# A fused encoder layer on one core: the even-block sums of a pair of products are made ahead of the decay scan

## What is computed

```python
h = rmsnorm(x, gains[2])
z = h @ w_in
q, fz, iv, og, u, ga, gb = jnp.split(z, IN_SPLITS, axis=-1)
logf = jnp.logaddexp(jnp.log(lb_h), jnp.log1p(-lb_h) + jax.nn.log_sigmoid(fz))
k = (1.0 - lb_h) * jax.nn.sigmoid(-fz)
# in chunks of 64 tokens, per head:
G = jnp.cumsum(gc, axis=-2)
o_inter = jnp.einsum('bhtk,bhkv->bhtv', qc * jnp.exp(G), S)
att = jnp.einsum('bhtk,bhsk,bhtsk->bhts', qc, kc, decay)
S_new = jnp.exp(G_last)[..., None] * S + einsum(kc * jnp.exp(G_last - G), vc)
```

## Time and profile before

| what | value |
|---|---|
| median of 3 runs | 2341.67 us (2340.02 to 2345.33) |
| the profiled execution | 2344.26 us |
| its span | 2342.5 us |
| TensorE busy, matmuls | 2270.4 us, 97% |
| VectorE busy | 1580.9 us, 67% |
| ScalarE busy | 1267.5 us, 54% |
| GpSimd busy | 1343.3 us, 57% |
| scans (line 2750) | 8, the first at 736.3, the last at 1119.3 us |

### The profile page before, as it was taken

The page is one execution under the profiler, slowest core; times in us unless marked ns, Lnnn a source line. Parts: engine busy times, 40 slices in busy tenths (PEclk is TensorE's granted clock), DMA queues, the critical chain, the costliest instruction groups (busy, mean ns, idle before and its releaser), DMA issues.

```text
span 2342.5 us, 54526 instructions
## 1 busy us (share of the span) xinstructions
PE 2270.4 (97%) x20432; PEld 1951.9 (83%) x20432; DVE 1580.9 (67%) x2618; ACT 1267.5 (54%) x2295; POOL 1343.3 (57%) x1019
## 2 busy tenths in 40 slices
PE   8899999999898999999999999999999999999998
PEld 6688888888787888888878888877888888888886
DVE  7877767635589788888982332389687777445755
ACT  6454555433576666666554434564555554334775
POOL 2787777767614555555645444306777778677120
PEclk9999999999999999999999999999999999999999
DMA  3123222443430111111121212331232222536202
GB/s 132 50 85 100 90 79 86 148 146 103 160 104 23 40 40 48 48 40 41 45 60 36 63 59 75 116 102 33 82 99 83 86 77 86 181 119 199 71 19 75
DMA packets 155236, 194.93 MB, mean 83 GB/s; under 512 B 13168, under 2 KB 102512, under 8 KB 155120
## 3 DMA queue, kind: packets, MB, share of 16 engines
q1 hardware_dynamic: 111920, 153.59, 20.7%
q10 hardware_dynamic: 43200, 39.83, 5.2%
HBM read 155.49 MB, written 37.88 MB: 83 GB/s over the span
## 4 chain that ended last, share of the span: by engine, by line
PE 72%; DVE 12%; POOL 5%; ACT 4%; issue 4%; DMA 2%; SPq 1%; ACTq 0%; DVEq 0%; POOLq 0%
PE bank L1069 18%; PE bank L1072 18%; PE bank L1071 18%; PE bank L1036 4%; PE bank L1038 4%; PE bank L1037 4%; POOL ring L930 2%; DVE hid L2204 2%; DMA ring<-weights 2%; POOL ring L934 1%; PE bank L1169 1%; DVE ops L2259 1%; DVE ops L2212 1%; DVE hid L2358 1%; PE bank L1204 1%
## 5 line engine op out<-in xcount | busy, mean ns | idle before, releaser
L1069 PE MATMUL bank<-ops,ring 128*128 128x264 f16 x4112 | 1138.0, 277 | 20.5 <-DVE ops L2368 7.4
L1071 PE MATMUL bank<-ops,ring 128*128 128x264 f16 x4112 | 1137.3, 277 | 0.0
L1072 PE MATMUL bank<-ops,ring 128*128 128x264 f16 x4112 | 1137.2, 277 | 0.0
L930 POOL TENSOR_TENSOR ring<-ring 128x512 f16<-128x512 f32 (+1 forms) x492 | 666.1, 1372 | 278.3 <-ACT ring L1404 278.3
L1404 ACT ACTIVATE ring<-ring 128x512 f16<-128x512 f32 (+1 forms) x492 | 286.4, 614 | 504.7 <-POOL ring L934 502.3
L1069 PEld LDWEIGHTS bank<-ops,ring 128*128 128x128 f16 x4112 | 404.0, 98 | 89.7 <-DVE ops L2368 8.5
L1072 PEld LDWEIGHTS bank<-ops,ring 128*128 128x128 f16 x4112 | 403.2, 98 | 61.2
L1071 PEld LDWEIGHTS bank<-ops,ring 128*128 128x128 f16 x4112 | 403.2, 98 | 59.9
L915 POOL TENSOR_TENSOR ring<-wtmp,ring 128x512 f16<-128x512 f32 x107 | 131.0, 1229 | 340.0 <-ACT ring L1345 339.4
L1036 PE MATMUL bank<-hid,ring 128*128 128x264 f16 x1068 | 294.9, 276 | 1.5 <-issue 1.3
L1038 PE MATMUL bank<-hid,ring 128*128 128x264 f16 x1068 | 294.8, 276 | 0.0
(11 more groups left out here) (227 smaller groups left out, 3627.5 us busy)
## 6 DMA issues: line engine op xcount, KB each, us to landing
ring<-weights SPq DMA_DIRECT2D x363, 256.0 KB, 2.8
ops<-spill SPq DMA_DIRECT2D x16, 1056.0 KB, 7.2
ring<-weights SPq DMA_DIRECT2D x120, 128.0 KB, 2.5
spill<-hid ACTq DMA_DIRECT2D x42, 264.0 KB, 2.9
spill<-hid ACTq DMA_DIRECT2D x20, 528.0 KB, 5.0
ops<-spill SPq DMA_DIRECT2D x8, 792.0 KB, 5.6
hid<-xT SPq DMA_DIRECT2D x8, 528.0 KB, 8.2
hid<-out_x ACTq DMA_DIRECT2D x8, 528.0 KB, 8.7
```

The costliest lines, as they stand in the source:

```text
L930: nc.gpsimd.tensor_tensor(low(slot, kh), weight_source(name, k, kh), high(slot, kh), ALU.subtract)\
L1069: nc.tensor.matmul(out, whi, xhi, start=(kk == 0 and fresh(name, k)), stop=False, skip_group_check=True)
L1071: nc.tensor.matmul(out, whi, xlo, start=False, stop=False, skip_group_check=True)
L1072: mm = nc.tensor.matmul(out, wlo, xhi, start=False, stop=end, skip_group_check=True)
```

## The change

On VectorE, in every turn but the first, the two sums of product 6 of the pair before now stand ahead of the wait for the logarithm and of the scan. The other engines' streams are the same.

```diff
+                if not (isinstance(h, int) and h == 1):
+                    sums_b_even("heads", h * 2 - 3, in_tokens(V))
                 dve.wait_ge(logf_ready, hh + 1)
                 V_.tensor_tensor_scan(GG, smask, W[2], 0.0, ALU.mult, ALU.add).then_inc(cum_ready, 1)
                 if isinstance(h, int) and h == 1:
                     t_lows(1, 4)
 
                     dve.wait_ge(t_ready, 14)
-                if not (isinstance(h, int) and h == 1):
-
-                    sums_b_even("heads", h * 2 - 3, in_tokens(V))
                 dve.wait_ge(cum_ready, hh + 1)
```

## The result

The changed kernel takes 2345.62 us in the median of 20 runs, the kernel before 2341.38 in 20 runs; the ratio is 1.0019 with a 95% interval of 1.0011 to 1.0026. Three of the forty runs (one before, two changed) were slow, at 2946 us and more; the ratio leaves them out, and without them the medians are 2345.01 and 2341.22. So the changed kernel is slower, by 3.8 to 4.2 us in the medians, which is 0.2%; the interval says 2.6 to 6.1 us.

What follows compares the result with a forecast made beforehand. TensorE (PE) bounds the kernel, busy 97% of the span and all 54.18 us of a head turn. Losses of 2.0 + 0.45 + 0.73 + 0.78 = 4.0 us on the 2341.67 median give 2345.7, range 2342.2 to 2348.0.

Steps and rivals of the forecast that it cites:

- Where the sums go: VectorE at the head seam: second sum starts 0.38 us after product 6's last matmul; V-transpose waits vanish, 1.4 us won.
- the lower bound: Changed turns gain their waits at the V transposes and lose nothing: -1.4 us.
- What is queued behind it: VectorE's scan, behind a sum waiting for PE, starts 1.08 us late; the difference L2760 starts 0.50 us late.
- Who waits for L2760: ACT, then POOL (4.32 us later), whose port lock sets the K operand's end (2.31 later); K-transpose wait 0.73 a turn.
- The sum: Turns 2 to 8 lose 2.0 + 0.45 + 0.73 + 0.78 = 4.0 us, won waits already set off.
- A turn: Sign of being right: one turn of the head loop takes 54.7 us in place of 54.18.
- B: Only VectorE's queue passes the delay to the K operand: 2.1 us slower, 2343.8; chance 0.17.
- C: K operand gets the shared port before POOL, both transpose waits vanish: 1.2 us faster, 2340.5; chance 0.09.
- D: L2760's bare wait on the scan's end costs 0.12 us a turn, 0.84 in all: +4.8, 2346.5; chance 0.27.
- E: Nothing moves, say because another wait sets the seam between heads: 2341.7; chance 0.05.

Runs made afterwards that it cites:

- experiment 1: Changed kernel, GpSimd waiting for VectorE's first operand before its last two subtractions of a pair; trace stretch 389.86 us (before 390.16, changed 394.17), turn 53.96.
- experiment 5: Changed kernel, ScalarE's two weight casts moved behind the copy of product 2; trace loop 323.77 us, stretch 388.16 (before 390.16).
- Experiment 3: Kernel before, VectorE waiting for both banks of product 6 ahead of the scan, sums still behind it; turn 54.91 us, stretch 395.7.
- experiment 4: Changed kernel, first sum ahead of the scan and second behind it; turn 54.32 us, trace stretch 390.89.
- experiment 7: Changed kernel with the sums ahead of the scan in turn 8 alone; trace loop 324.90 us, last stretch 66.03.
- experiment 6: Changed kernel, ScalarE's two weight casts moved ahead of the exponentials; turn 54.85 us (changed kernel 54.69).
- experiment 8: Changed kernel, casts behind the copy of product 2 in turns 2 to 7, turn 8 as before the change; 0.9996 of before, stretch 389.06 us.
- experiment 9: Changed kernel, casts behind the copy of product 2 in all turns, profiled again and timed; 2339.09 us, 0.999 of before, stretch 389.86.
- experiment 10: Kernel before, casts behind the copy of product 2, sums in the old order; 0.9995 of before, trace stretch 390.15 us.

## Why the prediction held

The forecast was 4.0 us and 2345.7; measured were 4.0 in the trace and 2345.62 in the runs. That the total fits to 0.1 us is in part luck: the medians scatter by more, and an excess of 0.05 in each wait was given back elsewhere (below). What carries weight is that the terms fit one by one.

- *Where the sums go.* The second sum starts 0.38 after the last matmul of product 6 (901.36, which is 904.06 less 2.70; the sum at 901.74). The wait at the V transposes went in all five turns. I had put it at 1.4 us. Its rows (0.34, 0.28, three times 0.27), less the 0.02 that is always there, sum to 1.3, and experiments 1 and 5 put its worth at 1.1 (324.88 less 323.77): part of such a wait is made up, since PE's nine loads right behind one take 0.94 in place of 0.99. The sum of 4.0 compares positions and does not use the 1.4; the lower bound does, and was too low by 0.3.
- *What is queued behind it.* The scan starts 0.73 after that matmul (0.71 predicted), the difference 3.17 (3.13 predicted). The missing 0.03 is the wait for the scan's own end, which I had counted as nothing: 902.09 + 2.41 = 904.50, and L2759 starts at 904.53. Experiment 3 shows that the wait for PE ahead of the scan is the cause; experiment 4 that a sum without such a wait costs next to nothing.
- *Who waits for L2760.* POOL starts 4.33 after it (4.32), the operand ends 2.30 after POOL's start (2.31), and PE's loads follow 0.06 later (0.05). Together 9.86 after the last matmul of product 6, where I had 9.81; against PE's bare 9.08 a wait of 0.78 in place of 0.73. The rows show 0.80 with the 0.02 that is always there.
- *The sum.* Turns 2 to 7 were to lose 2.0 + 0.45 + 0.73 = 3.18 and lost 3.28; turn 8 was to lose 0.78 and lost 0.73. The 0.05 a turn above would make 0.3 us in six turns; the first number is off by 0.1 only, since most was given back: behind its wait for the operand PE needs 47.53 us to the next V load (911.22 to 958.75), without one 47.58 (911.02 to 958.60 in experiment 5), so the wait of 0.78 costs a turn 0.73. That it comes out at the predicted number is luck; the prediction had no such term. In turn 8 VectorE is 0.83 late at the operand's end (counted from the V load) and 0.74 late where PE next stands for it (1.11 us at 1145.42), since its pair of operands before that takes 4.08 in place of 4.16. So its delay does come through, as predicted, but not whole.
- *A turn* of 54.7: measured 54.69. That turn 8 pays by itself, without the turns before it, experiment 7 shows.

The rivals. **B** (only VectorE's queue passes the delay on) is refuted by experiments 1 and 5: with VectorE as late as ever and the hold away, nobody waits. The Trainium skill's rule ("SBUF — State Buffer", section "SBUF: two separate sides"), an exclusive lock for the whole instruction, agrees with the trace in this: POOL's start plus a constant (2.30 or 2.31) set the operand's end in every turn from 2 to 8, before and after. That the first to start goes first does not describe experiments 1 and 6, where GpSimd came while VectorE was busy with the first of several such instructions: in 1 it stood behind four of them, in 6 behind one (last section). **C** (the port turns round) did not come: POOL led by 0.22 us in the loop (908.86 to 909.08), as counted. But experiments 1, 5 and 8 are C made by hand, and they give nearly what C was said to give: 1.1 us in the loop, where C had 1.2, and turns of 53.96. **D** (the bare wait on the scan's end costs 0.12) falls: it is 0.03, in the loop and in turn 8 alike (1120.86 + 2.42 = 1123.28, then 1123.31). The row I had taken it from (L2814, 0.12) also waits for the end of VectorE's own instruction before it, but for a bank of PE as well; why its gap is four times as long no run shows. **E** was refuted by the result.

Expectations failed on the way: that VectorE holds the port across two instructions (experiment 6), the gain of late casts in turn 8 (experiments 9, 10), which I had read from one profile, and with it the totals of experiments 1 and 5, whose last stretches came out at 66.09 and 64.39.

## What to carry to other kernels

Before an instruction is moved ahead of a wait, ask what it waits for itself: here the sum waited for PE longer than the wait it was moved past, and put a 2.4 us scan behind it. Follow such a delay beyond its own engine, since the price was set by a third one: ScalarE released GpSimd later, and GpSimd held VectorE's operand. And where an engine with work of no hurry sits on a port that a hurried one needs, ordering that work behind the hurried instruction can be worth more than either order of the rest (here 0.73 us a turn, against 0.52 between the two orders); it wants to be done only in the turns where nobody is late for it.

## What was not expected of the hardware

- A GpSimd instruction that came during one VectorE instruction ran ahead of the next, already queued one (L2694 took 2.25 in place of 1.28), while in another place it stood behind four (4.54 for one subtraction that takes 1.15 alone). The traces hold four such cases. GpSimd went next where it came 0.82 us after the start of the VectorE instruction (experiment 6: 904.23 against 903.41) and 0.86 after (experiment 10: 911.15 against 910.29). It stood until VectorE went to PSUM where it came 0.23 after (experiment 1: 910.00 against 909.77) and 0.25 after (experiment 5: 912.32 against 912.07). So it may be that one that comes early in an instruction loses its turn; no run was made to test that, and what decides is open.
- The same kernel kept the granted clock at 1.00 after PE had stood 2.38 us and went to 0.74 over 6.6 us after 2.40, which is 1.7 us in a stretch of 66. One profile of a kernel is one draw of such a step. Turn 1, which neither the change nor the late casts touch, has a like one behind PE's stand of 8.3 us: from those K loads to the V loads of turn 2 it took 48.86 us before, 49.65 changed and 50.38 in experiment 5, at granted clocks of 0.82, 0.75 and 0.66 over the first 8 or 9 us. Kernels before and changed have a step of that kind as well, behind the wait of 3.09 us in the gates. Their windows read 0.76 there, and neither the wait nor the step is touched by the change:

```profile
1187.90:1195.00 7.10, 7.08 (x49) 5.56 (x50) 6.57 (x9) 3.41 (x6) 4.16 (x3) 0.76 0.02 6
```

```profile
1187.90:1195.00 7.10, 6.15 (x40) 4.70 (x41) 6.53 (x12) 4.17 (x7) 4.38 (x3) 0.76 0.14 39
```
